# A two-block transformer kernel: the first four weight units after each norm run on one half of the tokens, then on the other

## The chip, the cores and the metric

One core of a Trainium2 chip runs the whole program. The metric is the time of the device in microseconds for one execution; the median of three runs of the kernel before is 858.37 us (857.8 to 862.53).

## What is computed

The reference is one layer each of two transformer blocks, one after the other, on 256 tokens of width 1024 in float32. Cut to what matters here:

```python
# first block
h = rmsnorm(x, attn_norm_w)                  # norm 0
proj = h @ w_in                              # q, k, v of both mixers, z, gates
o_la = gated_delta_rule(...)                 # after a causal conv of 4 taps and silu
o_d = diff_attention(...)
x = x + concat([o_la, o_d]) @ w_out
h = rmsnorm(x, ffn_norm_w)                   # norm 1
gate, up = split(h @ w_gate_up)
x = rmsnorm(x + (silu(gate) * up) @ w_down, final_norm_w)
# second block, with shifts and scales from mod = silu(c) @ w_ada + b_ada
h = rms_norm(x, g_pre_mix) * (1 + sc_m) + sh_m      # norm 2
y = token_mixer(h, w_in, ...)                # chunked attention, conv of 31 taps, two gates
x = x + gt_m * rms_norm(y, g_post_mix)
h = rms_norm(x, g_pre_ffn) * (1 + sc_f) + sh_f      # norm 3
x = x + gt_f * rms_norm(conv_ffn(h, w_up, w_dw, b_dw, w_down), g_post_ffn)
```

## The kernel before, in words

**Weights.** All large matrices come from HBM as a stream of units of 128 x 1024 float32 (512 KB). SP fetches each into one of six `raw` slots (`fetch`). ScalarE copies a unit into `whi`, rounded to the type fp32r; VectorE, or GpSimd for one unit in four of some stages, writes the rest into `wlo` (`prep`). There are five slots of each (`HL = 5`), and a unit's slot is free when TensorE is done with the unit five places ahead.

**Activations.** The normed input of a stage stands transposed in SBUF, again as two parts, `hh` and `hl`, each 128 partitions x 8 tiles x 256 tokens. A product is three matmuls: `hh` by `whi`, `hl` by `whi`, `hh` by `wlo`.

**The order of work.** `plan()` writes one list of steps, and every engine goes through the same list and issues its own part of each step, so the order in the list is the order in each engine's queue. `P.need(i, lead)` puts the `prep` steps in, up to `lead` units ahead. Banks of PSUM are handed over by semaphores (`full`, `free`).

**The steps around the change.** The norm of a stage is made in two blocks of 128 tokens. For a block, `sumsq` and `rows` scale the rows into `XN` (VectorE one half, ScalarE the other), and `turn` transposes them on TensorE (line 804), multiplies by the norm's weights on VectorE, rounds into `hh` on ScalarE and writes `hl` on VectorE. `turn(2n)` is block 0 and `turn(2n + 1)` block 1 of norm n. The step before (`last_four`) ends the stage before with four units on block 0 and then on block 1, with `turn(2n)` near its end. Then comes `first_four`: `turn(2n + 1)`, and two `pair`s of weight units. A pair fills one bank, 256 columns for each unit, in `stat`: the 128 x 128 tiles of the weights are loaded as the stationary operand and all 256 tokens move past. Eight tiles by three matmuls are 24 matmuls a unit and 96 for the four units:

```python
for k in range(4 * part, 4 * part + 4):
    w.wait_ge("h_hi", 4 * norm + 3 + k // 4)
    w.wait_ge("h_lo", 4 * norm + 3 + k // 4)
    a = whi[:, s, k * 128:k * 128 + 128]
    e.matmul(o, a, hh[:, k, :], start=(k == 0), stop=False)           # line 818
    e.matmul(o, a, hl[:, k, :], start=False, stop=False)              # line 819
    w.wait_ge(*P.lo_on[i])
    ins = e.matmul(o, wlo[:, s, ...], hh[:, k, :], ...)               # line 821
```

`first_four` is called four times: with `w_in` (norm 0; the convolutions of 4 taps, `conv`, read its banks), with `w_gate_up` (norm 1), with `w_in_2` (norm 2; before it stand `mod` and `gate_rows`, lines 1143 and 1151, in TensorE's queue) and with `w_up_2` (norm 3). The other 112 units of this kind go through `stat` with 256 tokens as well, and go on doing so.

Of the kernel before, what the change touches and what calls it, by code (L numbers as in the profile page):

```python
# [19 lines left out]
RAW, HL, LEAD = 6, 5, 3  # L20
# [176 lines left out]
def finish(gen):  # L197
    for _ in gen:
        pass
# [10 lines left out]
def plan():  # L210
    P = Plan()
    flags = set()

    def turn(t):
        for g in range(2):
            P.fill(f"turn{t}{g}")
        P.step("turn", t)

    def pair(tag, name, fs, src, kind="s"):

        bank = P.main % 2
        P.main += 1
        P.fill(tag, bank, frees=FREES.get(tag[:2], 1))
        for n, f in enumerate(fs):
            i = P.unit(kind, name, f)
            P.of[i] = (tag, n, src)
            P.step("stat" if kind == "s" else "whole", i, 0)
            yield
            P.step("stat" if kind == "s" else "whole", i, 1)
            if n == 0:  # L230
                P.uses(i)
                yield
            else:
                P.fills_bank(i, tag)
# [9 lines left out]
            P.fill(f"{tag}{n // 2}{n % 2}", first + n)  # L244

    def first_four(norm, tags, name, fs):
        turn(2 * norm + 1)
        for n in (0, 1):
            finish(pair(tags[n], name, fs[2 * n:2 * n + 2], ("h", norm)))

    def last_four(norm, tag, name, ks, src, block):
        ids = [P.unit("m", name, k, lead=0) for k in ks]
# [38 lines left out]
    P.need(0, lead=0)  # L291
    turn(0)
    first_four(0, ("cv0", "cv2"), "w_in", (0, 1, 2, 3))
    P.step("split_ba")
    P.step("conv", 0)
# [177 lines left out]
    P.step("tables")  # L473
    P.share = (0,)
    first_four(1, ("u10", "u11"), "w_gate_up", (0, FT, 1, FT + 1))
    ffn(1, None, "w_gate_up", "w_down", 1, 2, final_block, None)

# [3 lines left out]
    for n in range(4):  # L481
        P.fill(f"gt{n}")
    P.step("gate_rows")
    first_four(2, ("glu0", "glu1"), "w_in_2", (12, 16, 13, 17))
    P.side = [4, 5, 6, 7]
    P.step("biases2")
# [71 lines left out]
    for name, tag in (("w_attn_o_2", "ao"), ("w_conv_o_2", "co")):  # L558
        for u in range(4):
            P.fill(f"{tag}{u}", P.main % 2)  # L560
            P.main += 1
            i = P.unit("p", name, u)
# [28 lines left out]
FREES = {"qk": 2, "qq": 2, "gg": 2}  # L591
# [18 lines left out]
def program(nc, x_d, w_d, cols_d, const_d, bias1_d, bias2_d, rows_d, out_d):  # L610
    P = plan()
    units, place, F = P.units, P.place, P.fills
    NU = len(units)

    with ExitStack() as ctx:
        def sb(name, shape, dt=F32):
            return ctx.enter_context(nc.sbuf_tensor(name, shape, dt))

        raw = sb("raw", [128, RAW, 1024])
        whi = sb("whi", [128, HL, 1024], F32R)  # L620
        wlo = sb("wlo", [128, HL, 1024], F32R)
        X = sb("X", [128, 2, 1024])
        XN = sb("XN", [128, 2, 1024])
        hh = sb("hh", [128, KT, T], F32R)
        hl = sb("hl", [128, KT, T], F32R)
# [12 lines left out]
        banks = [ctx.enter_context(nc.psum_tensor(f"bank{i}", [128, 512], F32)) for i in range(8)]  # L638
# [28 lines left out]
        def tok(b):  # L667
            return slice(128 * b, 128 * b + 128)
# [77 lines left out]
        def fetched(i):  # L746
            return f"raw{i % RAW}", 16 * (i // RAW + 1)
# [26 lines left out]
        def _(e):  # L774
            w = Waits(e, sems)
# [4 lines left out]
            def open_bank(name):  # L780
                f = F[name]
                w.wait_ge(f.e, f.before)
                return banks[f.bank]

            def wait_after(name):
                w.wait_ge(F[name].e, F[name].after)

            def done(i, ins):
                ins.then_inc(sems[P.done[i][0]], 1)
# [17 lines left out]
            def stat(i, part):  # L807
# [14 lines left out]
                if part == 1:  # L822
                    done(i, ins)

            def whole(i, part):

                tag, n, _ = P.of[i]
                if n == 0 and part == 0:
                    open_bank(tag)
                o = banks[F[tag].bank][:, n * 256:n * 256 + 256]  # L830
                w.wait_ge(*fetched(i))
                for k in range(4 * part, 4 * part + 4):
                    wait_after(f"turn4{k // 4}")
                    wait_after(f"turn5{k // 4}")
                    ins = e.matmul(o, raw[:, i % RAW, k * 128:k * 128 + 128], h32[:, k, :], start=(k == 0), stop=(k == 7))  # L835
                if part == 1:
                    done(i, ins)
# [323 lines left out]
            def variance():  # L1161
# [4 lines left out]
                filled(ins, "var")  # L1166

            does = {
                "start": start, "turn": turn, "stat": stat, "whole": whole, "movv": movv, "mov": mov, "four": four, "ba": ba,
                "turn_ba": turn_ba, "lam": lam_, "norms": norms, "decay": decay, "kk": kk, "kq": kq, "lev_first": lev_first,  # L1170
                "lev_y": lev_y, "lev_tu": lev_tu, "vturn": vturn, "solve": solve, "cross": cross,
                "values_la": values_la, "head_la": head_la,
# [9 lines left out]
        def _(e):  # L1182
# [21 lines left out]
            def prep(i):  # L1204
                r = i % RAW
                if units[i][0] == "a":
                    _, k, c = units[i]
                    w.wait_ge(*fetched(i))
                    w.wait_ge("csilu", 1)
                    if k == 0:  # L1210
                        if c < 2:
                            w.wait_ge(F["turn01"].b, F["turn01"].full)
                            w.wait_ge(F["turn11"].b, F["turn11"].full)
                        else:
                            w.wait_ge(F["wo11"].b, F["wo11"].full)
                        ins = ts(ada_at[c], raw[:, r, :], csilu[:, k:k + 1], ALU.mult)
                    else:
                        w.wait_ge("ada", P.ada[i] - 1)
                        ins = stt(ada_at[c], raw[:, r, :], csilu[:, k:k + 1], ada_at[c], ALU.mult, ALU.add)
                    ins.then_inc(sems["ada"], 1)  # L1220
                elif i in P.lo_on and P.lo_on[i][0] == "lo_dve":
                    s = place[i] % HL
                    w.wait_ge("hi", place[i] + 1)
                    tt(wlo[:, s, :], raw[:, r, :], whi[:, s, :].bitcast(F32), ALU.subtract).then_inc(sems["lo_dve"], 1)
# [133 lines left out]
            def decay():  # L1358
                w.wait_ge("gate", GATE["m"])
                for x, (s, _) in enumerate(PAIRS):  # L1360
                    wait_after(f"D{x}")
                    tt(E[:, x, :, :], E[:, x, :, :], bc(mcol[:, 4 * s:4 * s + 4], 128), ALU.mult).then_inc(sems["em"], 1)
# [851 lines left out]
```

## Time and profile before

| what | value |
|---|---|
| median of three runs | 858.37 us |
| the profiled execution | 859.9 us |
| its span, first to last instruction | 858.1 us |
| TensorE busy (matmul) | 774.1 us, 90% |
| TensorE busy (weight load) | 703.9 us, 82% |
| VectorE, ScalarE, GpSimd busy | 585.2, 389.9, 133.0 us |
| mean granted TensorE clock | 0.953 |

The profile names each group by line, engine, operation and tile. PE is TensorE's matmul side and PEld its weight loads. Matmuls overlap in their pipeline, so that the distance between two starts, and not the length of one record, is what a matmul costs. The granted clock is 1.00 at full and 0.50 at half clock. A plain float32 matmul stands as two records (`mod` issues 16 at line 1143, and 32 are counted), one with fp32r operands, as in `stat`, as one. In the rows of stretches the columns are: the stretch; its length; busy us and instructions of PE, PEld, DVE, ACT, POOL; granted clock; DMA share; GB/s.

### The profile page before, as it was taken

How to read it: one execution, taken by the hardware profiler on the slowest of the kernel's cores; microseconds unless marked ns; L12 is line 12 of the kernel's file. 1: busy time of each engine (PE TensorE's matmuls, PEld its weight loads, DVE VectorE, ACT ScalarE, POOL GpSimd, SP SyncE). 2: the span in 40 equal slices, each digit the busy share in tenths (PEclk: the TensorE clock that was granted, in tenths of full speed). 3: DMA queues.
4: the chain of work that ended last, by engine and by line, in shares of the span. 5: the costliest groups of instructions: out<-in, count | busy, mean ns of one | idle time of the engine just before them, and what ended most of it. 6: DMA issues, size and time to landing. Idle time of an engine off the chain costs nothing.

```text
span 858.1 us, 13056 instructions
## 1 busy us (share of the span) xinstructions
PE 774.1 (90%) x5140; PEld 703.9 (82%) x5140; DVE 585.2 (68%) x935; ACT 389.9 (45%) x652; POOL 133.0 (16%) x76
## 2 busy tenths in 40 slices
PE   3969999798979999999978989999974999999995
PEld 2967898796779999999948978788964999999994
DVE  4675887555547868788757887556866576676664
ACT  5444223463435353534543434428353646555552
POOL 1202000002012222212232000000120121122220
PEclk9978999899879999999979999999996999999998
DMA  7662543233376888888823531344452355645531
GB/s 267 216 224 102 171 127 120 74 99 99 99 306 223 273 289 270 282 287 305 307 69 119 176 125 53 122 140 172 154 179 91 123 199 170 205 167 192 179 117 50
DMA packets 40382, 148.93 MB, mean 174 GB/s; under 512 B 4480, under 2 KB 4480, under 8 KB 39936
## 3 DMA queue, kind: packets, MB, share of 16 engines
q1 hardware_dynamic: 39456, 142.62, 49.3%
q10 hardware_dynamic: 864, 5.47, 1.6%
q8 instruction: 41, 0.67, 0.3%
q14 instruction: 21, 0.17, 0.1%
HBM read 147.02 MB, written 1.05 MB: 173 GB/s over the span
## 4 chain that ended last, share of the span: by engine, by line
PE 68%; DVE 11%; issue 10%; ACT 6%; POOL 3%; DMA 1%; POOLq 0%; DVEq 0%; ACTq 0%
PE bank L818 12%; PE bank L821 12%; PE bank L819 12%; PE bank L835 6%; PE bank L845 5%; PE bank L843 5%; PE bank L846 5%; PE bank L973 4%; ACT whi L1701 2%; DVE wlo L1196 2%; ACT XN L1701 2%; DVE arena L1202 2%; DVE XN L1202 2%; DVE arena L1196 2%; POOL small L1996 1%
## 5 line engine op out<-in xcount | busy, mean ns | idle before, releaser
L818 PE MATMUL bank<-hh,whi 128*128 128x256 f32 x1024 | 298.6, 292 | 12.1 <-ACT hh L1701 6.6
L819 PE MATMUL bank<-hl,whi 128*128 128x256 f32 x1024 | 295.1, 288 | 0.0
L821 PE MATMUL bank<-hh,wlo 128*128 128x256 f32 x1024 | 295.0, 288 | 0.0
L1196 DVE TENSOR_TENSOR wlo<-raw,whi 128x1024 fp32r<-128x1024 f32 x164 | 225.1, 1393 | 63.3 <-ACT whi L1701 63.0
L1701 ACT ACTIVATE whi<-raw 128x1024 fp32r<-128x1024 f32 x204 | 204.7, 1047 | 38.5 <-PE bank L821 17.4
L818 PEld LDWEIGHTS bank<-hh,whi 128*128 128x128 f32 x1024 | 202.0, 197 | 18.1 <-issue 15.1
L819 PEld LDWEIGHTS bank<-hl,whi 128*128 128x128 f32 x1024 | 202.2, 197 | 1.5
L821 PEld LDWEIGHTS bank<-hh,wlo 128*128 128x128 f32 x1024 | 201.9, 197 | 0.0
L1996 POOL TENSOR_TENSOR wlo<-raw,whi 128x1024 fp32r<-128x1024 f32 x40 | 105.4, 2636 | 474.8 <-ACT whi L1701 474.8
L1701 ACT ACTIVATE arena<-bank 128x256 f32<-128x256 f32 (+2 forms) x65 | 26.7, 420 | 115.3 <-PE bank L821 79.2
L1202 DVE SCALAR_TENSOR_TENSOR arena<-bank,cols,arena 128x255 f32<-128x255 f32 (+3 forms) x138 | 58.9, 479 | 26.7 <-ACT arena L1701 25.1
L843 PE MATMUL bank<-whi,fh 128*128 128x512 f32 x176 | 69.7, 396 | 2.1 <-ACT whi L1701 1.9
L845 PE MATMUL bank<-wlo,fh 128*128 128x512 f32 x176 | 69.8, 397 | 0.7 <-DVE wlo L1196 0.7
L846 PE MATMUL bank<-whi,fl 128*128 128x512 f32 x176 | 69.0, 392 | 0.0
L835 PE MATMUL bank<-arena,raw 128*128 128x256 f32 x256 | 59.5, 384 | 0.0
L1196 DVE TENSOR_TENSOR arena<-arena,bank 128x512 f32<-128x512 f32 (+1 forms) x57 | 32.4, 582 | 33.4 <-ACT arena L1701 23.9
L835 PEld LDWEIGHTS bank<-arena,raw 128*128 128x128 f32 x256 | 47.3, 190 | 8.0 <-issue 2.0
L1996 POOL TENSOR_TENSOR small<-small 128x1 f32<-128x1 f32 (+2 forms) x19 | 14.7, 773 | 241.4 <-DVE small L1199 154.7
L1202 DVE SCALAR_TENSOR_TENSOR XN<-arena,cols,XN 128x256 f32<-128x256 f32 x120 | 49.5, 480 | 0.0
L1196 DVE TENSOR_TENSOR fl<-arena,fh 128x256 fp32r<-128x256 f32 x48 | 21.7, 452 | 37.2 <-ACT fh L1701 37.2
L1202 DVE SCALAR_TENSOR_TENSOR arena<-raw,small,arena 128x1024 f32<-128x1024 f32 x28 | 46.5, 1660 | 0.3 <-DMA raw<-w_dram 0.3
L1701 ACT ACTIVATE arena<-arena 128x256 f32<-128x256 f32 (+1 forms) x45 | 19.3, 443 | 58.8 <-DVE arena L1202 58.2
(163 smaller groups left out, 943.0 us busy)
## 6 DMA issues: line engine op xcount, KB each, us to landing
raw<-w_dram SPq DMA_DIRECT2D x268, 512.0 KB, 4.4
arena<-rows_dram ACTq DMA_DIRECT2D x1, 1792.0 KB, 6.4
X<-x_dram SPq DMA_DIRECT2D x2, 512.0 KB, 6.3
arena<-rows_dram ACTq DMA_DIRECT2D x1, 1024.0 KB, 10.2
arena<-bias_dram ACTq DMA_DIRECT2D x1, 1024.0 KB, 13.0
out_dram<-X SPq DMA_DIRECT2D x4, 256.0 KB, 2.0
const<-const_dram ACTq DMA_DIRECT2D x1, 704.0 KB, 5.8
arena<-bias_dram ACTq DMA_DIRECT2D x1, 512.0 KB, 6.5
```

Of the source, the lines that this page charges most:

```text
L818: e.matmul(o, a, hh[:, k, :], start=(k == 0), stop=False)
L819: e.matmul(o, a, hl[:, k, :], start=False, stop=False)
L821: ins = e.matmul(o, wlo[:, s, k * 128:k * 128 + 128], hh[:, k, :], start=False, stop=(k == 7))
L835: ins = e.matmul(o, raw[:, i % RAW, k * 128:k * 128 + 128], h32[:, k, :], start=(k == 0), stop=(k == 7))
L843: e.matmul(o, lh[:, k, t0], whi[:, s, c:c + 512], start=first, stop=False)
L845: e.matmul(o, lh[:, k, t0], wlo[:, s, c:c + 512], start=False, stop=False)
L846: return e.matmul(o, ll[:, k, t0], whi[:, s, c:c + 512], start=False, stop=last)
L973: ins = e.matmul(p[:, h, :], lhs(h), rhs(h), start=True, stop=True)
L1196: return e.tensor_tensor(out, a, b, op)
L1202: return e.scalar_tensor_tensor(out=out, in0=a, scalar=s, in1=b, op0=op0, op1=op1)
L1701: return e.activation(out, a, func, scale=scale, **kw)
L1996: return e.tensor_tensor(out, a, b, op)
```

## The change

`first_four` is written anew. The four units' preparations stand ahead of `turn(2n + 1)`; all four units are then multiplied with tokens 0 to 127 alone (`half`, part 0), then comes `turn(2n + 1)`, and then the same four units are multiplied with tokens 128 to 255 (part 1). In both parts the same weight tiles are loaded. The waits of part 0 are on the first block of the norm, those of part 1 on the second.

```diff
     def first_four(norm, tags, name, fs):
+        ids = []
+        for tag in tags:
+            P.fill(tag, P.main % 2, frees=FREES.get(tag[:2], 1))
+            P.main += 1
+        for m, f in enumerate(fs):
+            i = P.unit("s", name, f, lead=0)
+            P.of[i] = (tags[m // 2], m % 2, ("h", norm))
+            ids.append(i)
+            P.step("half", i, 0)
         turn(2 * norm + 1)
-        for n in (0, 1):
-            finish(pair(tags[n], name, fs[2 * n:2 * n + 2], ("h", norm)))
+        for m, i in enumerate(ids):
+            P.need(i, lead=min(LEAD, m + 2))
+            P.step("half", i, 1)
+            if m % 2:
+                P.fills_bank(i, tags[m // 2])
+            else:
+                P.uses(i)
...
+            def half(i, b):
+                tag, n, (_, norm) = P.of[i]
+                s = place[i] % HL
+                if n == 0 and b == 0:
+                    open_bank(tag)
+                o = banks[F[tag].bank][:, n * 256 + 128 * b:n * 256 + 128 * b + 128]
+                w.wait_ge("hi", place[i] + 1)
+                for k in range(8):
+                    w.wait_ge("h_hi", 4 * norm + 2 * b + 1 + k // 4)
+                    w.wait_ge("h_lo", 4 * norm + 2 * b + 1 + k // 4)
+                    a = whi[:, s, k * 128:k * 128 + 128]
+                    e.matmul(o, a, hh[:, k, tok(b)], start=(k == 0), stop=False)
+                    e.matmul(o, a, hl[:, k, tok(b)], start=False, stop=False)
+                    w.wait_ge(*P.lo_on[i])
+                    ins = e.matmul(o, wlo[:, s, k * 128:k * 128 + 128], hh[:, k, tok(b)], start=False, stop=(k == 7))
+                if b == 1:
+                    done(i, ins)
```

## Rows read from the trace of the kernel before

**Rows 1.** The page, part 1: busy us, share of the span, instructions

```profile
PE 774.1 (90%) x5140; PEld 703.9 (82%) x5140; DVE 585.2 (68%) x935; ACT 389.9 (45%) x652; POOL 133.0 (16%) x76
```

**Rows 2.** What TensorE waited for: us in total, times, longest

```profile
PE bank L804 <- DVE XN L1199: 31.3, 6, 10.3
PE bank L939 <- DVE small L1196: 7.0, 1, 7.0
PE bank L818 <- ACT hh L1701: 6.6, 3, 2.6
PE bank L818 <- DVE hl L1196: 4.9, 1, 4.9
```

**Rows 3.** Timeline at norm 1: start, length, instruction, idle time before

```profile
235.47 1.29 DVE L1196 TENSOR_TENSOR hl<-arena,hh 128x512 fp32r<-128x512 f32 x2
...
240.29 1.94 PE L804 MATMUL bank<-const,XN 128*128 128x128 f32 x8 [6.26 <-DVE XN L1199]
...
243.71 0.55 PE L818 MATMUL bank<-hh,whi 128*128 128x256 f32 x1 [1.47 <-ACT hh L1701]
...
244.27 0.41 PE L821 MATMUL bank<-hh,wlo 128*128 128x256 f32 x1
244.48 0.41 PE L818 MATMUL bank<-hh,whi 128*128 128x256 f32 x1
...
257.30 0.28 PE L821 MATMUL bank<-hh,wlo 128*128 128x256 f32 x1
257.42 0.40 PE L843 MATMUL bank<-whi,fh 128*128 128x512 f32 x1
```

**Rows 4.** Stretches: busy time (instructions) of each engine, granted clock, DMA

```profile
236.10:243.70 7.60, 1.94 (x8) 1.59 (x9) 4.59 (x10) 3.39 (x8) 0.56 (x1) 0.65 0.61 223
437.30:439.60 2.30, 2.27 (x21) 2.28 (x21) 2.20 (x6) 1.26 (x2) 0.90 (x1) 1.00 0.68 239
439.80:441.80 2.00, 2.00 (x11) 2.00 (x11) 1.33 (x3) 1.23 (x4) 0.00 (x0) 0.50 0.53 205
455.10:466.60 11.50, 11.50 (x96) 11.50 (x97) 7.61 (x8) 4.28 (x5) 2.99 (x3) 1.00 0.53 156
641.90:645.00 3.10, 0.04 (x1) 0.00 (x0) 3.04 (x9) 1.26 (x3) 2.08 (x1) 0.92 0.49 169
```

**Rows 5.** Single lines: ns min/median/max, first and last start, shape

```profile
L1070 PE MATMUL bank<-const,arena x16: 164/250/250, 204.4 to 206.0; 128*128 128x1 f32 x16
...
L925 PEld LDWEIGHTS bank<-hh,wbh x8: 88/88/92, 44.6 to 47.0; 128*8 128x8 f32 x8
...
L819 PEld LDWEIGHTS bank<-hl,whi x1024: 187/192/338, 18.9 to 835.0; 128*128 128x128 f32 x171
...
L1143 PE MATMUL bank<-const,arena x32: 250/250/353, 437.3 to 441.8; 128*128 128x1 f32 x32
```

**Rows 6.** Groups by line: count, busy us, mean ns

```profile
L973 PE MATMUL bank<-arena 128*128 128x128 f32 x352 | 42.8, 278 | 0.0
```

**Rows 7.** Timeline at norm 0

```profile
13.62 3.03 DVE L1196 TENSOR_TENSOR hl<-arena,hh 128x512 fp32r<-128x512 f32 x2 [0.54 <-ACT hh L1701]
...
22.98 0.41 PE L819 MATMUL bank<-hl,whi 128*128 128x256 f32 x1
...
33.75 0.82 ACT L1701 ACTIVATE arena<-bank,cols 128x256 f32<-128x256 f32 x2
```

**Rows 8.** Timeline at norm 2

```profile
450.98 0.66 PE L804 MATMUL bank<-const,XN 128*128 128x128 f32 x4
...
455.08 0.36 PE L818 MATMUL bank<-hh,whi 128*128 128x256 f32 x1 [2.58 <-ACT hh L1701]
```

**Rows 9.** Timeline at norm 3

```profile
644.25 1.47 DVE L1196 TENSOR_TENSOR hl<-arena,hh 128x512 fp32r<-128x512 f32 x2
...
656.76 0.55 PE L818 MATMUL bank<-hh,whi 128*128 128x256 f32 x1 [2.57 <-ACT hh L1701]
...
670.34 0.28 PE L821 MATMUL bank<-hh,wlo 128*128 128x256 f32 x1
```

More of the change, by code:

```diff
@@ L1168, in _ @@
             does = {
-                "start": start, "turn": turn, "stat": stat, "whole": whole, "movv": movv, "mov": mov, "four": four, "ba": ba,
+                "start": start, "turn": turn, "stat": stat, "half": half, "whole": whole, "movv": movv, "mov": mov, "four": four, "ba": ba,
                 "turn_ba": turn_ba, "lam": lam_, "norms": norms, "decay": decay, "kk": kk, "kq": kq, "lev_first": lev_first,
```

## The prediction

> **What bounds the kernel now.** I read the busy times first, then TensorE's waits, then the timeline around each of the four norms. TensorE is busy for 774.1 of 858.1 us [rows 1], so the kernel is TensorE's length plus the places where it idles. The longest waits are those of the transposes (line 804) for the normed rows, 31.3 us in six places, and those of the first weight matmuls for `hh` and `hl`, 6.6 and 4.9 us [rows 2]. That is the time the change goes after. Norm 1 shows its form [rows 3]: `hl` of block 0 is written from 235.47 (its first half to about 236.15), the transposes of block 1 start only at 240.29 after 6.26 us of idleness, and the first of the 96 weight matmuls at 243.71. In between TensorE has nothing but the eight transposes, although the first 128 tokens are ready from 236.15. The four units end at 257.42.
>
> **Part 1: what a matmul of 128 tokens costs.** This decides the sign. With 256 tokens the starts lie 0.12 us apart at full clock (257.30, 257.42) and 0.21 at half clock (244.27, 244.48) [rows 3]. The trace has no fp32r matmul with 128 moving columns. The change issues 192 matmuls in place of 96 in each stage, each with its own load of 128 x 128 weights. The rows on the load: a load of 8 columns takes 88 ns, one of 128 columns 192 ns [rows 5], which makes (192 - 88) / 120 = 0.87 ns a column, or 0.11 us for 128 beyond the fixed part. And where the moving side has one column, line 1070, 16 records start between 204.4 and 206.0 [rows 5]: 1.6 / 15 = 0.107 us apart, so the load alone sets that pace. For 128 columns line 973 has 42.8 / 352 = 0.122 us a record [rows 6]. At half clock it doubles: of the 32 one-column records of line 1143 (437.3 to 441.8) [rows 5] some 21 lie in the 2.3 us at full clock [rows 4], and the last ten or so take 2.1 us, 0.21 each.
>
> So I take 0.12 us at full and 0.21 at half clock for a matmul of half the tokens: the same as for all of them. Splitting the tokens saves nothing per matmul and doubles their number. The lower bound is 0.066 us, where only the columns count (0.12 less half of 256 columns at 2.4 GHz, 0.053). The upper bound is that of plain float32, two records of line 973 for one matmul, 0.24 us. The value taken is the one whose rows hold the same weight load.
>
> The Trainium skill speaks for the lower bound: TensorE: Matmul & The Clock Gate, section "Back-to-back issue gap", gives about 81 ns a matmul for a stream of loads and matmuls with 128 columns. By 0.081 instead of 0.12 the eight half passes would cost 8 x 96 x 0.039 = 30 us less (an estimate from that page). No run here has such a matmul.
>
> **Part 2: the clock.** TensorE was at full clock before norm 1 ended its work at 234.0, and the stretch from 236.10 has a mean granted clock of 0.65, so that it fell after (0.65 - 0.5) / 0.5 x 7.6 = 2.3 us, at 238.4 [rows 4]. It came back to full 4.8 us after the first weight matmul: 22 of these cost 0.09 us more than they would, 2.0 us. At norm 0 the matmul of 22.98 still takes 0.41 us, so the 4.4 us before were at half clock too [rows 7]. A TensorE whose queue is full can lose its clock as well: in 437.30 to 439.60 it is busy for 2.27 of 2.30 us with one-column matmuls at 1.00, and from 439.80 it is at 0.50, just as busy [rows 4]. A half pass moves columns for 0.053 us in each 0.12, or 0.107 in each 0.21 at half clock. It lies between that stretch and the full-width stream of 455.10 to 466.60, which stays at 1.00 [rows 4]. I take it that a half pass which starts at half clock stays there to its end, and that one which starts at full clock keeps it until an idle gap comes.
>
> By the Trainium skill, TensorE: Matmul & The Clock Gate, section "The HAM clock gate", activity releases the throttle and idleness brings it back; read as "matmuls back to back are activity", the half passes would run at full clock soon after they start. The trace's one-column stretch is against such a reading. What that would give is the second case below.
>
> **Part 3: the four stages.** A half pass is 96 matmuls: 11.5 us at full, 20.4 at half clock (0.2125 each, as at 244).
> - Norm 0: `hl` of block 0 and the first `wlo` are there at about 16 [rows 7], the clock is low. Pass 0 to 36.4; the transposes queued behind it 1.9; the way through VectorE and ScalarE 1.5 (as in 242.2 to 243.71 [rows 3]), to 39.8; pass 1 to 60.2. The convolution of the second pair, which began at 33.75 [rows 7], begins then: 26.5 us later. From there VectorE leads, and TensorE waits 7.0 us for it at line 939 [rows 2], which hides the slow restart. I take +27.
> - Norm 1: pass 0 from 236.15, 18 matmuls before 238.4 and 78 at half clock, to 254.9; transposes 1.94, idle 1.47, to 258.3; pass 1 to 278.7; 2.0 lost until the clock is back. 280.7 against 257.4: +23.3.
> - Norm 2: `mod` and `gate_rows` stand ahead of it in TensorE's queue until 450.98, whatever is ready [rows 8]. Pass 0 from 451.0 at full clock to 462.5; transposes 1.5, idle 2.58 while VectorE scales eight tiles, to 466.6. That idle gap, after a pass that moves columns half the time, takes the clock: pass 1 to 487.0, and 2.0 more: 489.0 against 466.6: +22.4.
> - Norm 3: `hl` of block 0 is there at 645.0, after 3 us of idleness in which the clock falls (0.92 over 641.90 to 645.00) [rows 4, 9]. Pass 0 to 665.4, transposes 1.94, idle 2.57, to 669.9, pass 1 to 690.3, and 2.0: 692.3 against 670.5 (the last matmul starts at 670.34): +21.8.
>
> Behind norms 1, 2 and 3 come stages where TensorE is the bound, so nothing there gives it back. The sum is 27 + 23.3 + 22.4 + 21.8 = 94.5 us.
>
> **The edits that cost nothing.** The four preparations are now ahead of `turn(2n + 1)` on ScalarE, VectorE, GpSimd and SP. At norms 1 to 3 only one unit is left to prepare then (a copy of 1.0 us and a subtraction of 1.2, or 2.4 on GpSimd), and `turn`'s work on these engines now waits behind the transposes, which wait behind pass 0: 11 to 20 us of cover. At norm 0 it is three units, 3.5 us of VectorE, under the same cover, with the first due 5 us after pass 0 starts. If pass 0 took no time, up to these 3.5 us would show. SP's fetches come no later than before up to the fourth unit. While pass 0 runs no slot is freed, so the next fetches pause for up to 20 us; six loaded slots and 24 matmuls per unit in pass 1 cover that at 4.4 us a load.
>
> The profiled execution took 859.9 us, 1.5 above the median of 858.4. 859.9 + 94.5 = 954.4 there, and 953 against the median.
>
> **The rivals.**
> - The clock stays up, or comes up as before: the pace is 0.12 us except for 4.5 us at norms 0 and 3. For it: the transposes and pass 0 leave gaps of only 2 to 3 us, and a pass moves columns far more than the stretch of rows 4. Norm 0: pass 0 to 29.4, pass 1 from 32.0 to 43.5, +9.8. Norm 1: to 247.7, 250.2, 261.7: +4.3. Norm 2: 462.5, 466.6, 478.1: +11.5. Norm 3: 658.6, 662.2, 673.7: +3.2. Together +29: 887.
> - A narrow fp32r matmul goes at plain float32's pace, 0.24 us, with the array occupied and the clock up: a pass of 23 us. Norm 0 +32, norm 1 236.15 + 23 + 2.5 + 23 = 284.7, +27.3; norm 2 451 + 23 + 4.1 + 23, +34.5; norm 3 645 + 23 + 5.6 + 23, +26. Together +120: 978. Against it: operands that need no second record before should need none now.
> - The other side, faster: the pace is that of the columns, 0.066 us, a pass of 6.4. Norm 1: 236.15 + 6.4 + 2.5 + 6.4 = 251.5, -5.9. Norm 3: with 4.7 us at half clock to 653.1, then 656.8 and 663.2, -7.3. Norm 2 +1.3, as nothing waits there for block 0; norm 0 about 0. Together -12: 847. It decides in the other direction once a narrow matmul costs under about 0.09 us with the clock up. Against it are the rows of the load [rows 5, 6]. This is where the page's 81 ns belongs.
> - The idleness between the blocks is worth less than it looks: part of norm 2's case already, where pass 0 can't start before 451.0.
>
> **How the numbers follow.** 0.50 for the forecast (953; its own range, for where in a pass the clock falls, 930 to 965), 0.25 for the clock staying up (887, or between it and the forecast), 0.13 for plain float32's pace, 0.09 for the columns' pace, 0.03 for something not named here that leaves it within 5 us. A measurement of this kernel tells about 0.5% from no change. The range of 8 in 10 takes in the second case and most of the third: 880 to 980. Faster 0.09, same 0.03, slower 0.88.
>
> **What would show it.** The starts of lines 818 to 821's successors in `half`: 0.12 or 0.21 us apart as here, 0.066 or 0.24 by the rivals. Granted clock 0.50 over most of 16 to 60 and of the 40 us behind norm 1. TensorE's busy time up by the whole of the loss, and its waits at line 804 nearly gone. The prediction is wrong if narrow matmuls start less than 0.1 us apart at full clock, or if the clock is at 1.00 through pass 1.

## The result and the profile after

The changed kernel takes 951.7 us (median of four runs, 950.41 to 952.66); the kernel before took 859.43 beside it. The ratio is 1.107, interval 1.103 to 1.111: slower by 92 us. The forecast was 953. The profiled execution spans 948.6 us, 90.5 more than before, at a mean granted clock of 0.902 where it was 0.953.

The page, part 1, of the changed kernel, answering to [rows 1]:

```profile
PE 876.5 (92%) x5524; PEld 806.3 (85%) x5524; DVE 585.1 (62%) x935; ACT 390.7 (41%) x652; POOL 134.1 (14%) x76
```

TensorE has 384 more matmuls and is busy for 102 us more; the other engines have what they had. What TensorE waited for (us in total, times, longest), answering to [rows 2]; line 819 is the transpose now, line 852 the first matmul of a tile in `half`:

```profile
PE bank L819 <- DVE XN L1233: 14.2, 3, 9.4
PE bank L852 <- ACT hh L1735: 11.6, 5, 3.1
PE bank L852 <- DVE hl L1230: 7.4, 2, 5.1
PE bank L973 <- DVE small L1230: 5.2, 1, 5.2
```

The transposes' wait fell from 31.3 to 14.2 us. What is left is ahead of block 0 (9.4 us at the start of the kernel, 2.7 at norm 3, 2.1 at norm 2); none is ahead of block 1, so the change did what it says. The matmuls' own waits for the norm rose from 11.5 to 19.0, since the stages now wait once for each block (norm 2 for the second only). Norm 1 in the timeline, answering to [rows 3]:

```profile
262.15 0.27 PE L853 MATMUL bank<-hl,whi 128*128 128x128 f32 x1
262.26 0.28 PE L855 MATMUL bank<-hh,wlo 128*128 128x128 f32 x1
...
280.16 0.41 PE L853 MATMUL bank<-hl,whi 128*128 128x128 f32 x1
280.38 0.41 PE L855 MATMUL bank<-hh,wlo 128*128 128x128 f32 x1
280.59 1.93 PE L819 MATMUL bank<-const,XN 128*128 128x128 f32 x8
...
283.99 0.45 PE L852 MATMUL bank<-hh,whi 128*128 128x128 f32 x1 [1.47 <-ACT hh L1735]
...
304.29 0.41 PE L855 MATMUL bank<-hh,wlo 128*128 128x128 f32 x1
304.50 0.73 PE L877 MATMUL bank<-whi,fh 128*128 128x512 f32 x1
```

A matmul of 128 tokens starts 0.11 us after the last at full clock and 0.21 at half, like one of 256. The stretches show the clock (busy us and instructions of PE, PEld, DVE, ACT, POOL; granted clock; DMA), answering to [rows 4]. The passes are those of norms 0 (two lines), 1 (four), 2 (three) and 3 (two):

```profile
16.50:36.90 20.40, 20.40 (x96) 20.40 (x96) 3.84 (x4) 0.73 (x1) 0.00 (x0) 1.00 0.33 104
40.40:59.10 18.70, 18.70 (x96) 18.70 (x97) 5.84 (x10) 6.07 (x10) 2.36 (x1) 0.55 0.36 113
...
262.00:264.40 2.40, 2.39 (x21) 2.40 (x21) 1.66 (x3) 1.30 (x4) 0.00 (x0) 0.95 0.46 176
264.60:282.00 17.40, 17.40 (x83) 17.40 (x84) 2.10 (x4) 1.78 (x2) 0.56 (x1) 0.50 0.64 257
284.00:304.50 20.50, 20.50 (x96) 20.50 (x97) 3.85 (x5) 3.66 (x5) 2.36 (x1) 0.50 0.24 78
304.50:308.80 4.30, 4.30 (x12) 3.38 (x13) 3.09 (x5) 2.70 (x4) 0.73 (x1) 0.53 0.06 12
500.00:511.00 11.00, 11.00 (x98) 10.76 (x98) 2.10 (x3) 0.00 (x0) 3.50 (x2) 1.00 0.13 49
...
515.00:517.00 2.00, 2.00 (x17) 2.00 (x18) 1.74 (x2) 0.84 (x1) 0.00 (x0) 0.93 0.00 0
517.20:533.80 16.60, 16.60 (x80) 16.60 (x80) 4.57 (x5) 2.48 (x3) 2.94 (x3) 0.50 0.30 96
714.60:735.00 20.40, 20.39 (x96) 20.40 (x97) 5.60 (x9) 4.20 (x10) 1.11 (x2) 0.50 0.16 52
739.50:760.00 20.50, 20.46 (x96) 20.49 (x97) 5.64 (x9) 6.05 (x8) 2.37 (x1) 0.50 0.26 78
```

TensorE is busy without a break in each of them, and at half clock in all but pass 0 of norm 2 and the first microseconds of three others. For pass 0 of norm 0 that is read from the spacing alone: 96 matmuls in 20.4 us are 0.213 us each, but the profile's granted clock says 1.00 there, as it does for all of the first 42 us. The kernel before shows the same (clock 1.00 at norm 0, with matmuls 0.213 us apart until 23.2), so that the mean clocks of both kernels come out too high.

### The profile page after: what moved, and what is told of

The parts are those of the page before. It is cut to its first block, busy times and chain, and to the rows that moved or that the text cites. A ratio compares the mean times of both kernels' runs of the same rounds, so it can differ in the third digit from the quotient of the medians.

```text
span 948.6 us, 13832 instructions
## 1 busy us (share of the span) xinstructions
PE 876.5 (92%) x5524; PEld 806.3 (85%) x5524; DVE 585.1 (62%) x935; ACT 390.7 (41%) x652; POOL 134.1 (14%) x76
## 4 chain that ended last, share of the span: by engine, by line
PE 72%; issue 10%; DVE 10%; ACT 5%; POOL 2%; DMA 1%; POOLq 0%; DVEq 0%; ACTq 0%
PE bank L833 10%; PE bank L836 10%; PE bank L834 10%; PE bank L869 6%; PE bank L879 5%; PE bank L852 5%; PE bank L877 5%; PE bank L880 5%; PE bank L853 5%; PE bank L855 5%; PE bank L1007 4%; DVE wlo L1230 2%; ACT whi L1735 2%; DVE arena L1236 2%; DVE arena L1230 1%
## 5 line engine op out<-in xcount | busy, mean ns | idle before, releaser
L833 PE MATMUL bank<-hh,whi 128*128 128x256 f32 x896 | 260.8, 291 | 0.0
L834 PE MATMUL bank<-hl,whi 128*128 128x256 f32 x896 | 257.7, 288 | 0.0
L836 PE MATMUL bank<-hh,wlo 128*128 128x256 f32 x896 | 257.6, 288 | 0.0
L1735 ACT ACTIVATE whi<-raw 128x1024 fp32r<-128x1024 f32 x204 | 205.1, 1047 | 57.2 <-PE bank L855 31.3
L833 PEld LDWEIGHTS bank<-hh,whi 128*128 128x128 f32 x896 | 176.4, 197 | 4.3 <-issue 2.2
L834 PEld LDWEIGHTS bank<-hl,whi 128*128 128x128 f32 x896 | 176.3, 197 | 1.5
L836 PEld LDWEIGHTS bank<-hh,wlo 128*128 128x128 f32 x896 | 176.1, 197 | 0.0
L852 PE MATMUL bank<-hh,whi 128*128 128x128 f32 x256 | 99.7, 389 | 19.0 <-ACT hh L1735 11.6
L855 PE MATMUL bank<-hh,wlo 128*128 128x128 f32 x256 | 99.5, 389 | 0.0
L853 PE MATMUL bank<-hl,whi 128*128 128x128 f32 x256 | 99.4, 388 | 0.0
L852 PEld LDWEIGHTS bank<-hh,whi 128*128 128x128 f32 x256 | 77.8, 304 | 21.9 <-ACT hh L1735 9.8
L853 PEld LDWEIGHTS bank<-hl,whi 128*128 128x128 f32 x256 | 78.3, 306 | 0.2 <-issue 0.2
L855 PEld LDWEIGHTS bank<-hh,wlo 128*128 128x128 f32 x256 | 78.5, 306 | 0.0
```

The costliest lines, as they stand in the source:

```text
L836: ins = e.matmul(o, wlo[:, s, k * 128:k * 128 + 128], hh[:, k, :], start=False, stop=(k == 7))
L852: e.matmul(o, a, hh[:, k, tok(b)], start=(k == 0), stop=False)
L853: e.matmul(o, a, hl[:, k, tok(b)], start=False, stop=False)
L855: ins = e.matmul(o, wlo[:, s, k * 128:k * 128 + 128], hh[:, k, tok(b)], start=False, stop=(k == 7))
L1735: return e.activation(out, a, func, scale=scale, **kw)
```

## The experiments

**The order without the halves.** From the changed kernel:

```diff
-            P.step("half", i, 0)                 # ahead of turn
-            P.step("half", i, 1)                 # behind it
+            P.step("stat", i, 0)
+            P.step("stat", i, 1)
```

> The change without its half passes: the four units' preparations stand ahead of the transposes of block 1 as in the changed kernel, and the units are then multiplied once with all 256 tokens. Theory (the loss is all in the half passes): the time of the kernel before, 859 us within 0.4%. Rival (the moved preparations or the queue order cost something, since ScalarE, VectorE and SP now pass four units ahead of the norm): 5 to 15 us above it, seen as waits of TensorE for hh or hl at norms 0 and 1.

Measured: 869.65 us against 858.41, ratio 1.013 (1.011 to 1.015). The theory fell and the rival came true: the moved preparations cost 11 us by themselves. The timeline of this kernel at norm 1:

```profile
245.40 1.06 ACT L1735 ACTIVATE whi<-raw 128x1024 fp32r<-128x1024 f32 x1 [0.69 <-issue]
246.48 1.22 DVE L1230 TENSOR_TENSOR wlo<-raw,whi 128x1024 fp32r<-128x1024 f32 x1 [2.02 <-ACT whi L1735]
247.63 1.28 DVE L1230 TENSOR_TENSOR arena<-bank,cols 128x512 f32<-128x512 f32 x2
...
249.84 0.55 PE L833 MATMUL bank<-hh,whi 128*128 128x256 f32 x1 [3.29 <-DVE hl L1230]
```

VectorE splits the next unit before it scales the transposed block, and TensorE waits 3.29 us where it waited 1.47 [rows 3]. At norm 0 there are three units ahead, and the first weight matmul starts at 22.25, 3.5 us late. In the changed kernel this work lies under pass 0: there the wait ahead of pass 1 is 1.47 again at norm 1 and 2.57 as before at norm 3, and at norm 2 the first matmul comes 4.04 us after the start of the transposes where it was 4.10. So the 11 us are not part of the 92, but they are what the cover is worth.

**As many matmuls, full width.** From the changed kernel:

```diff
-                o = banks[F[tag].bank][:, n * 256 + 128 * b:n * 256 + 128 * b + 128]
+                o = banks[F[tag].bank][:, n * 256:n * 256 + 256]
+                def both(h, k):
+                    return h[:, k, :] if b else rep(h[:, k, tok(0)], 2)
...
-                    e.matmul(o, a, hh[:, k, tok(b)], start=(k == 0), stop=False)
+                    e.matmul(o, a, both(hh, k), start=(k == 0), stop=False)
```

> The changed kernel with as many matmuls and weight loads, but each of them 256 columns wide: pass 0 moves the first 128 tokens twice (the second copy is overwritten later), pass 1 moves all 256 tokens. Theory (a half pass costs one load a matmul whatever the columns, and it holds the clock at half because it moves few columns): the pace stays 0.12 us at full clock and the clock comes back within 5 us of the start of a pass, so that only the doubled count is left: 859 + 29 = 888 us, 880 to 895. Rival A (columns cost too, since a matmul is load plus columns): 888 + 768 x 0.05 = 926 or more. Rival B (the clock is low because of the order of the passes and the gap between them, not because of the width): 952 us as the changed kernel.

Measured: 899.24 us, ratio 1.048 (1.045 to 1.051), 52 us below the changed kernel with twice the columns. Four of its eight passes:

```profile
247.50:259.10 11.60, 11.58 (x96) 11.60 (x97) 3.61 (x6) 3.12 (x6) 0.56 (x1) 1.00 0.73 274
262.00:275.00 13.00, 13.00 (x96) 13.00 (x97) 3.63 (x5) 3.45 (x5) 2.37 (x1) 0.87 0.46 161
676.20:689.20 13.00, 13.00 (x97) 13.00 (x98) 5.57 (x9) 4.17 (x10) 1.11 (x2) 0.88 0.26 80
693.20:706.20 13.00, 12.99 (x96) 13.00 (x96) 5.53 (x9) 6.03 (x8) 2.42 (x1) 0.87 0.30 94
```

A pass takes 11.6 us, or 13.0 where the clock fell in the gap ahead of it, and not 20.5. Both rivals fall: A asked for 926 or more, B for 952. This splits the loss: about 40 us for the second set of 96 matmuls in each stage, about 52 for the clock that narrow ones behind full loads don't bring back. It is 11 us above the 888 expected, and above that range's end of 895. The profiled execution, with a span of 895.1 (37 over that of before, against 29), shows where 8 of them are: the stages cost 11.4, 5.9, 13.9 and 5.8 us, where 9.8, 4.3, 11.5 and 3.2 were counted. About 1.4 us at each of norms 1, 2 and 3 is the clock, which falls at the gap between the passes and is low for about 3.4 us; the rest of the 8, and what two of the other runs lost (they took 901 us), is not accounted for.

**Half passes at one norm.** The code of before at all norms but one:

```diff
     def first_four(norm, tags, name, fs):
+        if norm not in (3,):                     # or (2,)
+            turn(2 * norm + 1)
+            for n in (0, 1):
+                finish(pair(tags[n], name, fs[2 * n:2 * n + 2], ("h", norm)))
+            return
```

> Half passes at norm 3 alone, the code of before at norms 0 to 2. Theory (each stage pays for itself and nothing behind it gives anything back): 21 us over the kernel before, 880 us, with two passes of 96 matmuls 0.213 us apart at granted clock 0.50. Rival (the stages share one cost, as a clock that once lowered stays lower for long, or slots running late): clearly more or less than a quarter of the 92 us, under 870 or over 890.

> Half passes at norm 2 alone, where pass 0 ran at full clock in the changed kernel. Theory: 20 us over the kernel before, 880 us: pass 0 0.12 us a matmul at clock 1.00, then 3 us of idleness, and pass 1 at 0.213 for most of its length. Rival (the clock falls in pass 0 by itself, whatever gap follows): granted clock 0.50 already within pass 0 and about 28 us over.

Measured: 880.73 us at norm 3 (ratio 1.026, 1.024 to 1.028) and 881.24 at norm 2 (1.025, 1.022 to 1.028), both as the theory has it. Norm 3's two passes, then norm 2's two in the other kernel:

```profile
646.00:666.50 20.50, 20.40 (x96) 20.43 (x96) 5.64 (x9) 4.28 (x11) 1.11 (x2) 0.50 0.16 52
671.00:691.50 20.50, 20.39 (x96) 20.43 (x96) 5.65 (x9) 6.11 (x9) 2.36 (x1) 0.50 0.23 78
```

```profile
449.20:460.30 11.10, 11.10 (x99) 10.86 (x98) 2.68 (x3) 0.00 (x0) 3.71 (x3) 1.00 0.15 49
465.70:483.50 17.80, 17.80 (x86) 17.80 (x85) 4.72 (x6) 2.48 (x3) 3.10 (x3) 0.50 0.28 90
```

Each of the two costs about a fourth of the whole; norms 0 and 1 were not run alone. Pass 0 of norm 2, with no gap ahead of it, keeps the full clock to its end, so the rival (the clock falls within it) is out. Pass 1, after a gap of 3.0 us, starts at full clock and loses it within 2 us.

**What sets the pace.** Two kernels from the changed one. In the first, two matmuls of three load 64 of the 128 weight columns (the other half of their output is left out). In the second, two of three move 64 of the 128 tokens (the products of the other tokens are left out). One of the two matmuls is shown, the one with `wlo` is cut in the same way; in the first kernel the matmul with the full load also moves to the end of the last tile:

```diff
-                    e.matmul(o, a, hl[:, k, tok(b)], start=False, stop=False)
+                    e.matmul(o[0:64, :], a[:, 0:64], hl[:, k, tok(b)], start=False, stop=False)           # first
+                    e.matmul(o[:, 0:64], a, hl[:, k, 128 * b:128 * b + 64], start=False, stop=False)      # second
...
```

> The changed kernel, but two of the three matmuls of each tile (hl by whi and hh by wlo) load only 64 of the 128 weight columns, and so leave out half of their output rows; the moving side keeps 128 tokens. Theory (the weight load of 128 columns sets the pace): those two go at some 0.067 us at full and 0.107 at half clock, the third at 0.12 and 0.213, on average 0.085 and 0.142: 768 x 0.07 = 54 us less than the changed kernel at an unchanged clock, 898 us, and down to 880 if the clock comes up. Rival (a fixed price of every narrow matmul, not its load): the same 952 us.

> The changed kernel, but two of the three matmuls of each tile (hl and wlo) move only 64 of the 128 tokens and so leave out half of their products; all loads stay at 128 columns. Theory (the load sets the pace): the starts stay 0.12 us apart at full and 0.213 at half clock, the time is that of the changed kernel, 952 us, or up to 9 us more where the clock of norm 2's pass 0 falls as well. Rival (columns are part of the price): the two matmuls gain 0.027 us each at full and 0.053 at half clock, 512 x 0.045 = 23 us less, 929 us.

Measured: 874.28 us (1.020, 1.018 to 1.022) for the short loads, 959.89 (1.117, 1.114 to 1.121) for the short moves. The first kernel at full clock:

```profile
472.01 0.28 PE L853 MATMUL bank<-hh,whi 128*128 128x128 f32 x1
472.13 0.23 PE L854 MATMUL bank<-hl,whi 128*64 128x128 f32 x1
472.19 0.22 PE L856 MATMUL bank<-hh,wlo 128*64 128x128 f32 x1
472.25 0.28 PE L853 MATMUL bank<-hh,whi 128*128 128x128 f32 x1
```

And the second, the first matmul of four tiles, two at full clock and two at half:

```profile
505.71 0.31 PE L852 MATMUL bank<-hh,whi 128*128 128x128 f32 x1
506.05 0.31 PE L852 MATMUL bank<-hh,whi 128*128 128x128 f32 x1
...
507.85 0.45 PE L852 MATMUL bank<-hh,whi 128*128 128x128 f32 x1
508.49 0.45 PE L852 MATMUL bank<-hh,whi 128*128 128x128 f32 x1
```

With 64 weight columns a matmul costs 0.06 us, from its start to the next, instead of 0.11, and the three of a tile 0.24; with 64 tokens three of them still take 0.34 us, 0.11 each, and at half clock 0.64, 0.21 each. The load is the price and the moving columns are free below it. The first kernel comes out under its expectation of 898 because its clock comes up (0.958 in the mean, 0.902 in the changed kernel); the expectation had that as its lower end, 880, and the kernel is 6 us below it. Its pass 0 at norms 1 and 3:

```profile
240.30:250.50 10.20, 9.33 (x96) 9.06 (x96) 3.55 (x6) 3.12 (x6) 0.56 (x1) 0.83 0.72 269
655.20:666.40 11.20, 10.72 (x96) 10.58 (x96) 5.59 (x9) 4.19 (x10) 1.10 (x2) 0.70 0.20 54
```

At norm 3 the pass starts at half clock (a tile of three matmuls takes some 0.43 us) and from about 661.8 on runs at full (0.23), while it moves 128 tokens a matmul, as the changed kernel does. So narrowness alone doesn't hold the clock down: narrow matmuls behind full loads do, and behind half loads the clock comes back.

The second kernel is 8 us above the changed kernel: its clock falls within pass 0 of norm 2 with no gap there, at about 507. The expectation had allowed up to 9 us for that.

**Matmuls that nobody reads.** If idleness takes the clock, then filling it should give time to the kernel before:

```diff
+WARM = {0: (0, 5), 1: (44, 9), 2: (0, 0), 3: (78, 18)}
...
     def first_four(norm, tags, name, fs):
+        P.step("warm", norm, bank, P.nfree[bank], ahead)
         turn(2 * norm + 1)
+        P.step("warm", norm, bank, P.nfree[bank], behind)
...
+                        e.matmul(banks[bank][:, 0:256], mh[:, k, 0:128], mh[:, k, :], start=True, stop=True)
```

> The kernel before, with matmuls whose result nobody reads put into the idle places of TensorE: 256 columns wide, 44 ahead of and 9 behind the transposes of block 1 at norm 1, 78 and 18 at norm 3, and 2 and 5 plain float32 ones at norm 0. Theory (the clock falls because the array moves nothing there, and its return costs 2.0 us at each place): granted clock 1.00 from the norm on, transposes 0.9 us shorter at norms 1 and 3, together 2.0 + 2.9 + 2.9 = 7.8 us less, 851 us. Rival (the clock falls for another reason, or the added work delays the transposes): 859 us or more.

Measured: 853.37 us, ratio 0.9933 (0.9908 to 0.9957). It beats both kernels, by 5.4 us of median against the kernel before, where 7.8 were expected. Norm 1 and norm 3 in its profile:

```profile
230.32 5.44 PE L820 MATMUL bank<-mh 128*128 128x256 f32 x44
...
236.72 1.06 PE L812 MATMUL bank<-const,XN 128*128 128x128 f32 x8 [0.96 <-DVE XN L1216]
```

```profile
243.00:247.00 4.00, 4.00 (x36) 4.00 (x35) 1.43 (x2) 2.18 (x3) 0.81 (x1) 1.00 1.00 415
640.00:652.00 12.00, 10.41 (x86) 10.02 (x85) 8.43 (x19) 5.10 (x12) 1.10 (x2) 1.00 0.16 56
```

The clock stays at 1.00 through both norms, and the transposes take 1.06 us where they took 1.94 [rows 3]. The span of the profiled execution is 6.7 us shorter; the clock fell for 3.4 us at norm 2 instead. A second set fills that place too:

> The kernel with the unread matmuls, and 18 more behind the transposes at norm 2, where TensorE waits 2.6 us and its clock fell for 3.4 us in the profile. Theory: the clock stays at full there, up to 1.6 us less than with the earlier set, 852 us. Rival (that fall costs nothing on the path, or comes only in some executions): 853.4 again.

Measured: 852.3 us, ratio 0.990 (0.988 to 0.993). The clock holds at norm 2, but the two sets' intervals overlap, so the last microsecond isn't shown. In the profiled execution of this kernel the matmuls at norm 0 run 0.213 us apart until about 24.6, in that of the first set 0.12 from the start, though both have the same added matmuls there: at norm 0 they don't always hold the clock.

**gate_rows behind norm 2's first units**, in the kernel with the unread matmuls:

> As the kernel before with the unread matmuls, and gate_rows moved behind the first four units of norm 2. Theory: gate_rows held the transposes of block 1 from 446.6, where their rows are ready, to 450.98; moved, they start 4 us sooner at half clock, and gate_rows' eight records cost 2 us later: some 2 us less than with the unread matmuls alone, 849 us. Rival (VectorE and GpSimd, which make gate_rows' results, are late for the next stage): no gain or up to 5 us more.

Measured: 860.17 us, ratio 1.001 (1.000 to 1.002), 7 us worse than with the unread matmuls alone: the rival, and 2 us beyond its upper end. TensorE finishes the four units sooner and then waits for results that VectorE and GpSimd make behind `gate_rows`:

```profile
PE bank L835 <- DVE arena L1219: 4.0, 1, 4.0
```

Behind this wait the clock is low again from 467.6 to 470.9.

**One unit of four in halves.** This is the change with the added matmuls cut to what the idleness holds:

> Half passes for the first of the four units only, so that the added 24 matmuls (2.9 us at full clock, 5.1 at half) fit into the idleness before the transposes at norms 1 and 3 (4.1 and 7.2 us from the time block 0 is ready); the other three units as before. Theory (a half pass costs what a full one costs, so that a split never shortens what is left after the transposes, and costs its extra matmuls where no idleness covers them): nothing at norms 1 and 3, some 3 us at norm 0 (3 of 5.1 us fit there), 3 us and up to 2 for the clock at norm 2, whose queue is full: 860 to 866 us. Rival (there is something to win, as the design assumes): under 855 us.

Measured: 874.13 us, ratio 1.016 (1.012 to 1.020). There is nothing to win this way, as the theory says, but the loss is 8 us beyond the upper end of its 860 to 866. In the trace, from pass 0 to pass 0, norm 0 gives 8.9 of the 15.1 us (3 expected): the rows for block 1's transposes were ready at 12, and even 24 matmuls at half clock, from 16.27, put them off to 21.43. Norm 2 gives 6.0 (3 to 5 expected), norms 1 and 3 give 0.2 and nothing.

```profile
16.27 0.44 PE L849 MATMUL bank<-hh,whi 128*128 128x128 f32 x1 [5.08 <-DVE hl L1227]
...
21.43 1.93 PE L816 MATMUL bank<-const,XN 128*128 128x128 f32 x8
```

## Why the prediction was right

**The price of a narrow matmul.** Taken at 0.12 and 0.21 us, measured at 0.11 and 0.21. The rivals of 0.066 and 0.24 us are both out. The Trainium skill's 81 ns (TensorE: Matmul & The Clock Gate, "Back-to-back issue gap") doesn't hold for these fp32r operands. The break-even that the prediction puts at about 0.09 us comes out at 0.082 from its own two cases (+29 us at 0.12, -12 at 0.066); nothing hangs on it here. That it is the load was argued from one-column rows of plain float32 [rows 5]; the two kernels with 64 columns show it for fp32r.

**The clock.** That a half pass starting at half clock stays there was the riskiest step. It held in the four passes that started so (the first at norm 0, the second at norm 1, both at norm 3), and the three that began at full clock behind an idle gap lost it within 2.5 us and stayed low. At norm 1 the clock is low from 264.5 to 308.8, through 44.3 us in which TensorE is busy for 42.8. What the prediction had not foreseen is that at norm 0 the clock came up between the passes. The kernel with full-width passes shows what the low clock is worth, some 52 us, and that at full loads the width decides; the one with 64 weight columns, where it came up within narrow passes, that the width doesn't decide alone. The reading of the Trainium skill's page (TensorE: Matmul & The Clock Gate, section "The HAM clock gate") by which matmuls back to back are activity enough falls with the 44.3 us, since TensorE was fed without a break in both passes.

**The stages**, from the shift of the same point in the two traces (the start of pass 0 at norms 1 to 3, as 262.01 against 236.15, and the end):

| norm | forecast, us | measured, us | what was off |
|---|---|---|---|
| 0 | 27 | 25.9 | clock up for the first 2 us of pass 1 |
| 1 | 23.3 | 23.0 | |
| 2 | 22.4 | 20.7 | pass 0 at 0.11, not 0.12, a matmul; clock up for the first 2 us of pass 1 |
| 3 | 21.8 | 20.9 | clock back 2.5 us after the passes, so that 1.3 and not 2.0 us were lost |
| sum | 94.5 | 90.5 | |

Each stage was taken 0.3 to 1.7 us too high. That 953 lies within 1.3 us of 951.7 is in part luck: the medians are 92.3 us apart against 94.5, and the kernel before took 1 us more beside the changed one than in the forecast.

One sign could not be read as the prediction named it: the granted clock of the profile is 1.00 until 42, not 0.50 from 16 on. The spacing of the matmuls shows the half clock there.

**The edits costed at nothing.** Right, with pass 0 as their cover. The forecast's word that up to 3.5 us would show without it held at norm 0 (3.5), but it was short elsewhere: the one unit left at norms 1 to 3, for which it named no price, puts the first matmul off by 1.1 to 1.8 us. These and the 3.5 make 7.5 of the 11. Some 2 us more are the clock at norm 2: the weight matmuls start there at half clock and keep it until about 467.5, where the kernel before had the full one. The rest was not traced.

**The idleness.** As forecast, TensorE's busy time rose by more than the loss (102 of 90 us) and no wait is left ahead of a block 1.

## What to carry to other kernels

A stationary operand that is loaded for each matmul has a price of its own, here that of 256 moving fp32r columns at 128 weight columns: splitting the moving side below that saves nothing and doubles the loads, so that here the cover of a norm costs more than the wait that it fills (moving the weights past the tokens instead, as other units of this kernel do, was not tried here). Narrow matmuls behind full loads may also fail to bring TensorE's clock back, so that a stream with no gaps runs at half clock for 20 us; with loads of half the size the clock came back. Where TensorE idles ahead of a long full-width stretch, unread full-width matmuls in the gap are worth trying: 0.7% here (0.4 to 0.9).

## What the runs showed that was not expected

- At norm 0 the clock came up between the passes: pass 0 ran at 0.213 us a matmul to its end, and after the eight transposes pass 1 began at 0.12, with a mean of 0.55 over its length (the line of 40.40). I had it at half throughout. In the kernel that moves 64 tokens in two of three matmuls pass 1 began there at half clock. What brought it up is open.
- A load of 64 columns gives half the price: 0.06 us at full and some 0.11 at half clock.
- With two of three matmuls moving 64 tokens the clock fell in the middle of a stream that had no gap; with 128 tokens it held for 96 matmuls.
